# Norming the first token tile by itself at the start of a two-layer trunk, with its loads in another order

## The reference

```python
def layer_norm(x, g, b, eps=1e-5):
    mu = mean(x); var = mean((x - mu) ** 2)
    return (x - mu) * rsqrt(var + eps) * g + b

h = layer_norm(x, ln_in_g, ln_in_b)
for l in range(DEPTH):
    proj = h @ w_in[l]          # 1024 x N_IN, then the three mixers
    ...
```

## Time and profile before

| | before |
|---|---|
| median of 3 runs | 1507.97 us (1507.71 to 1509.43) |
| span of the profiled execution, first to last instruction | 1504.3 us |
| PE busy | 1442.3 us, 96% |
| DVE busy | 752.0 us, 50% |
| ACT busy | 584.0 us, 39% |
| read from HBM | 471.53 MB, 314 GB/s over the span |

### The profile page before, as it was taken

One profiled execution on the slowest core, in us unless ns is written; L12 is line 12 of the kernel. 1 busy time (PEld: TensorE's weight loads), 2 busy tenths in 40 slices (PEclk: granted clock), 3 DMA queues, 4 the chain that ended last, 5 costly groups with the idle time before them and its releaser, 6 DMA issues.

```text
span 1504.3 us, 17635 instructions
## 1 busy us (share of the span) xinstructions
PE 1442.3 (96%) x7456; PEld 993.6 (66%) x7456; DVE 752.0 (50%) x791; ACT 584.0 (39%) x621; POOL 13.3 (1%) x18
## 2 busy tenths in 40 slices
PE   8999999999999999999999899999988999999876
PEld 7987888888888988886343478863423688734223
DVE  7449687555557548674112079941110598510103
ACT  4357665344335357751100067730000577400001
POOL 1000010000000000010000000000000000000000
PEclk9999999999999999999999999999999999999999
DMA  9253275555554353289999999999999999999995
GB/s 358 108 224 126 98 252 204 187 193 179 187 196 168 113 224 127 98 333 430 430 430 429 428 431 430 429 406 431 429 431 430 429 431 428 420 430 431 429 430 228
DMA packets 43245, 473.70 MB, mean 315 GB/s; under 512 B 5424, under 2 KB 5552, under 8 KB 7712
## 3 DMA queue, kind: packets, MB, share of 16 engines
q1 hardware_dynamic: 42336, 467.97, 76.6%
q0 software_dynamic: 832, 4.63, 0.8%
HBM read 471.53 MB, written 1.05 MB: 314 GB/s over the span
## 4 chain that ended last, share of the span: by engine, by line
PE 68%; DMA 17%; DVE 9%; ACT 4%; issue 2%; DVEq 0%; SPq 0%; ACTq 0%
PE ps L1939 15%; PE ps L1940 15%; PE ps L1941 15%; PE ps L2366 12%; DMA raw_b<-in_w_item 11%; DMA raw_a<-in_w_item 6%; PE ps L2403 5%; DVE lo_a L1233 2%; PE ps L2323 1%; ACT w_hi L847 1%; PE ps L2373 1%; ACT prob_even L966 1%; PE ps L1969 1%; DVE small_mix L1449 1%; DVE lo_b L1656 1%
## 5 line engine op out<-in xcount | busy, mean ns | idle before, releaser
L1233 DVE TENSOR_TENSOR lo_a<-raw_a,w_hi 128x2048 fp32r<-128x2048 f32 (+1 forms) x109 | 239.9, 2211 | 120.6 <-ACT w_hi L847 120.0
L1939 PE MATMUL ps<-w_hi,act_hi 128*128 128x512 f32 (+1 forms) x640 | 246.1, 385 | 2.7 <-DVE act_lo L1347 1.1
L847 ACT ACTIVATE w_hi<-raw_a 128x2048 fp32r<-128x2048 f32 (+1 forms) x109 | 200.8, 1848 | 114.2 <-PE ps L1941 113.9
L1941 PE MATMUL ps<-w_hi,act_lo 128*128 128x512 f32 (+1 forms) x640 | 242.5, 379 | 0.0
L1940 PE MATMUL ps<-lo_a,act_hi 128*128 128x512 f32 (+1 forms) x640 | 242.5, 379 | 0.0
L2366 PE MATMUL ps<-raw_a,x_small 128*64 128x512 f32 (+1 forms) x784 | 150.7, 534 | 7.3 <-DMA raw_a<-in_w_item 7.3
L2366 PE MATMUL ps<-raw_b,x_small 128*64 128x512 f32 (+1 forms) x704 | 140.2, 546 | 9.5 <-DMA raw_b<-in_w_item 9.5
L1135 ACT ACTIVATE hidT<-ps 128x512 f32<-128x512 f32 (+1 forms) x24 | 13.0, 544 | 324.3 <-PE ps L2373 324.3
L1939 PEld LDWEIGHTS ps<-w_hi,act_hi 128*128 128x128 f32 x640 | 120.4, 188 | 27.7 <-issue 2.1
L1941 PEld LDWEIGHTS ps<-w_hi,act_lo 128*128 128x128 f32 x640 | 120.4, 188 | 23.0
L1940 PEld LDWEIGHTS ps<-lo_a,act_hi 128*128 128x128 f32 x640 | 120.5, 188 | 21.2
(11 more groups left out here) (293 smaller groups left out, 1905.1 us busy)
## 6 DMA issues: line engine op xcount, KB each, us to landing
raw_a<-in_w_item SPq DMA_DIRECT2D x83, 2048.0 KB, 22.0
raw_b<-in_w_item SPq DMA_DIRECT2D x81, 2048.0 KB, 22.6
raw_a<-in_w_mix SPq DMA_DIRECT2D x60, 1024.0 KB, 4.9
raw_a<-in_w_item SPq DMA_DIRECT2D x43, 1024.0 KB, 5.1
raw_a<-in_w_mix SPq DMA_DIRECT2D x8, 512.0 KB, 3.7
ln_gb<-in_ln_mix POOLq DMA_DIRECT2D x2, 1024.0 KB, 5.6
raw_x<-in_w_item SPq DMA_DIRECT2D x1, 2048.0 KB, 17.3
raw_act<-in_w_item SPq DMA_DIRECT2D x1, 2048.0 KB, 19.7
```

What stands on the lines that cost most here:

```text
L847: nc.scalar.activation(w_upper(g)[:, 0:n], raw(slot)[:, 0:n], ACT.Copy).then_inc(s_hi, 1)
L1233: nc.vector.tensor_tensor(w_lo(slot)[:, 0:n], raw(slot)[:, 0:n], w_upper(g)[:, 0:n].bitcast(F32), ALU.subtract).then_inc(s_lo, 1)
L1939: nc.tensor.matmul(dst, xh, wh, start=start, stop=False)
L1941: return nc.tensor.matmul(dst, xl, wh, start=False, stop=stop)
```

## The change

SP issues tile 0 of x, the identity, `ln_gb`, weight unit 0 and then tile 1 of x; units 1 to 3 follow. DVE computes statistics, variance and refinement for tile 0 alone and normalises it, and only then does statistics and variance of tile 1 (`first_statistics(1)`), all of it ahead of the lower part of tile 0. The refinement for tile 1 stands in `first_normalise(1)`, at its old place. ACT takes two roots of one column each; the second stands between the pieces 1 and 2 of unit 0. PE's order is as before.

```diff
             sp.dma_start(ident, consts[:, 0:P]).then_inc(s_id, 16)
+            sp.dma_start(ln_gb[:], ln_in.rearrange("(o m) d -> o m d", o=1).to_broadcast([P, 2, D])).then_inc(s_gbf, 16)
+            first_load(0)
             sp.dma_start(h[:, 1, :], x[0, P:2 * P]).then_inc(s_x[1], 16)
-            sp.dma_start(ln_gb[:], ln_in.rearrange("(o m) d -> o m d", o=1).to_broadcast([P, 2, D])).then_inc(s_gbf, 16)
-            for k in range(4):
+            for k in range(1, 4):
                 first_load(k)
...
             act.wait_ge(s_idle, 1)
             ready_root()
-            root(TILES)
+            root(1)
             transposed_hi(0, act_hi, (0,))
             first_split(0)
             first_split(1)
+            root(1)
             transposed_hi(0, act_hi, (1,))
...
+            def first_statistics(t):
+                dve.wait_ge(s_x[t], 16)
+                for b in range(2):
+                    statistics(h, t, b)
+                link(nc.vector.bn_aggr(mv[:, t, :], bst[:, t].rearrange("p c m -> p (c m)")))
+                nc.vector.tensor_scalar(rv[:, 0:1], mv[:, t, 1:2], 1e-5, 0.25, ALU.add, ALU.mult).then_inc(s_rv, 1)
+
             def first_normalise(t):
                 halves = [slice(0, 512), slice(512, 1024)]
+                refine(1, rn[:, t:t + 1])
+                dve.wait_ge(s_gbf, 16)
                 for cols in halves:
...
-            for t in range(TILES):
-                dve.wait_ge(s_x[t], 16)
-                for b in range(2):
-                    statistics(h, t, b)
-                link(nc.vector.bn_aggr(mv[:, t, :], bst[:, t].rearrange("p c m -> p (c m)")))
-            nc.vector.tensor_scalar(rv[:, 0:TILES], mv[:, :, 1], 1e-5, 0.25, ALU.add, ALU.mult).then_inc(s_rv, 1)
-            refine(TILES, rn[:, 0:TILES])
-            dve.wait_ge(s_gbf, 16)
+            first_statistics(0)
             first_normalise(0)
+            first_statistics(1)
             transposed_lo(0, act_hi, act_lo, (0,))
```

## The result

| | before | changed |
|---|---|---|
| median, first measurement | 1508.07 us (11 runs, 1505.92 to 1509.43) | 1512.14 us (11 runs, 1508.35 to 1514.06) |
| ratio, 95% interval, first measurement | | 1.0020 (1.0011 to 1.0029) |
| second measurement, another chip | 1508.54 us (29 runs) | 1511.18 us (12 runs), 1.0018 (1.0009 to 1.0027) |
| third measurement, a third chip | 1508.10 us (35 runs) | 1510.48 us (12 runs), 1.0016 (1.0005 to 1.0027) |
| span of the first profile | 1504.3 us | 1510.9 us |

The changed kernel is slower, by 2.4 to 3.0 us by the three ratios (0.0016 to 0.0020 of 1508). The forecast was +1.0, 1509.0 with a range up to 1510.5; the first median, 1512.14, lies outside of it.

What follows compares the result with a forecast made beforehand. PE was taken to bound the kernel, so a late start counts in full. Landing of tile 1 of x plus 6.24 put its norm 0.98 us late: span 1504.3 + 1.0 = 1505.3, plus 3.67 gives 1509.0 us, range 1507.7 to 1510.5.

Steps and rivals of the forecast that it cites:

- the gain on tile 0: On DVE, tile 0's normalising begins at 8.25 us instead of 9.96, 1.7 us earlier.
- the block of six: Six DVE instructions from the first `act_lo` to tile 1's second refinement, taken to last 3.61 us.
- the step that carries the delay one to one: No engine has room behind the start, so a late start moves both later stages by the same time.
- it lands at 8.15 to 8.6, I take 8.2: Landing of `ln_gb` in the new load order, in us, with 1.64 MB up to its end.
- I take 11.9, the measured landing of exactly those bytes: Landing of tile 1 of x, in us, closing the same five transfers that weight unit 0 closed before.
- The late bound of 12.35 for the landing: Tile 1 of x landing 1.45 us behind its bytes, at 12.35 us; the sum is then +1.4 us.
- the term "landing": Landing of tile 1 of x, taken as 11.9 us; tile 1's norm on DVE starts 6.24 us after it.
- the lowest run (-0.3): Lower end of the range, from a start level with the kernel before and the lowest run: 1507.7 us.
- The first (an early landing): Tile 1 of x lands by or before the end of tile 0's norm; +0.2, 1508.2 us, chance 0.15.
- the fourth (the earlier tile 0 wins): The stream is set by tile 0's products, not tile 1's norm; 1.4 us gained, 1506.6 us, chance 0.04.
- The second (absorbed later): A fixed resource behind the start ends last and absorbs the delay; 1508.0 us, chance 0.07.
- The third (the clock falls): PE, idle 2.6 us ahead of the first product, drops to its lower clock; +3.7, 1511.7 us, chance 0.04.

Runs made afterwards that it cites:

- late_stats: The changed kernel with tile 1's statistics and variance moved behind the four pieces of unit 0, ACT's second root behind its piece 3; ratio 1.0021 to the kernel before.
- order_only: The changed order on DVE and ACT, with the loads in the order of the kernel before; ratio 1.0007 to the kernel before.
- x_fourth: The changed kernel with tile 1 of x issued ahead of weight unit 0, behind `ln_gb`; ratio 1.0002 to the kernel before.
- after_third: The changed kernel, not edited, measured a third time; ratio 1.0016 to the kernel before.
- loads_only: The loads in the changed order, with the order on DVE and ACT of the kernel before; 1513.8 us, ratio 1.0032 to the kernel before.
- before_again: The kernel before, not edited, measured and profiled again; ratio 1.0006.
- split_refine: Loads as before; each tile refined separately, both refinements and tile 1's statistics placed in DVE's idle times; ratio 1.0005 to the kernel before.

## Why the prediction was wrong

**Right: what decides.** The stream's start is set by tile 1's norm on DVE; the gain on tile 0 is lost; a wait of 0.8 us for tile 1 of x stands ahead of its statistics (0.78 measured); the block of six takes 3.6, the refinement 0.65 (3.60 and 0.64). The sign was right, and so was the step that carries the delay one to one, as far as 523 us. That the wait came out although both landings were missed is no luck: tile 1 of x lands 3.6 to 3.7 us behind `ln_gb` in all seven profiles with the new loads, tile 0's norm takes 2.87 of this, and in the six with the new order on DVE the wait is 0.71 to 0.79.

**Wrong: the landings, of `ln_gb` and with it of tile 1 of x.** The steps "it lands at 8.15 to 8.6, I take 8.2" and "I take 11.9, the measured landing of exactly those bytes" failed. In the seven profiles with the new loads (late_stats apart, where they stand elsewhere) its statistics start between 12.15 and 13.92, 12.97 on average; 11.97 was the estimate. The late bound of 12.35 for the landing was too tight as well. In the four profiles with the first five transfers in the old order and 1 MB of `ln_gb` the fifth lands at 11.9 to 12.7. So the same bytes in another order land later, by some 0.7 us on average, though the two ranges overlap and the profiles are few; the runs do not show the reason. The other 0.35 is that the profile used was the earliest of the four. All of it is there at `ln_gb`, which closes the first 1.64 MB: 8.45 to 10.15 us in the seven profiles, 9.2 on average, where 8.2 was taken.

**Wrong: the sum, in consequence.** Tile 1's norm starts at 18.16 to 19.93 in the profiles with the new loads and the changed order on DVE, 18.90 on average over the six with tile 1's statistics in the changed place: 1.75 us late, not 0.98. At equal clock the changed kernel is 1.7 and 1.8 us slower in its two paired measurements, and about 2.4 in the first by the pooled level of before (1503.9 against 1506.3). The mechanism was right and the term "landing" was mis-sized, by 1.4 us in the first profile and by about 0.9 on average over the six; the terms behind it, 6.24 in the sum, were 0.15 too long, since statistics and variance take 1.77 and not 1.90.

**Wrong: what the loss was put down to.** The prediction spoke of the wait and of what is queued behind it. order_only and x_fourth show that the wait itself is the smaller part, 0.86 us: the statistics, variance and refinement of tile 1 were hidden in the time in which DVE waited for `ln_gb` anyway, and the change put them on the path. From norm to norm it takes 9.66 us instead of 7.19, which is 2.47 more: 1.77 for statistics and variance, 0.64 for the refinement, 0.78 for the wait, less the 0.71 of idle time ahead of the first `act_lo` that they fill. Against that stands the earlier start of tile 0's norm, 0.34 us in the first profile and up to 1.39 in after_third (8.57).

**Wrong: the range.** It took the noise from three runs that were 1.7 us apart and from one profile with a mean clock of 0.998. That step ("the lowest run (-0.3)", "the upper spread of the runs") failed: the kernel's runs spread over 7 us, with the granted clock. Of the 4.1 us between the first two medians, some 2 are the start. By the 0.49 another 0.7 is clock (10.8 us lost in the 11 changed runs, 9.3 on average over the 99 of the kernel before); the granted clock of the runs it was paired with is not known. The rest is chance as far as is known: the means of the same runs are only 3.5 us apart, and later pairs 2.6 and 2.4 at the median. Whether a part of it belongs to the change (the changed kernel lost 10.8, 10.2 and 10.7 us of clock time, the kernel before 9.6, 8.9, 9.5, but 10.8 in before_again) is left open: it would be worth about 0.5 us.

**The rivals.** The first (an early landing) and the fourth (the earlier tile 0 wins) did not come. The second (absorbed later) holds in part: loads_only was 6.9 us late at tile 1's norm and 5.2 at the end on average, and the profiles regain 1.3 to 4.1 us behind 746 us. For the changed kernel itself it did not help: 1.75 us late at the norm, 1.7 and 1.8 slower at equal clock. The third (the clock falls) had 0.04 and came in one profile of three, at a price of 0.5 us at the stream, not 3.7, since the waits for DVE hid most of it. The page on the clock gate ("TensorE: Matmul & The Clock Gate", "Part 1: The HAM clock gate", of the Trainium skill) says that idle time lets the clock fall; the traces agree that it can after 2.38 us (2.48 in late_stats, 7.6 in loads_only), and show that it need not after 2.38 or 3.23.

## What to carry to other kernels

Before you split a joint step so that the first part can start early, look at what the joint step was hidden behind: here one engine computed both tiles' statistics while it waited for a load anyway, and splitting put 2.4 us of its work and a wait onto the path, 2.5 more in all between the two norms, to win at most 1.4. If you split, place each new piece in a named idle time of that engine (split_refine: level, where the change lost 2). And take the noise from many runs with their granted clock; three runs and one profile can all be lucky.

## What the runs showed of the hardware

- The granted clock differs between executions of one kernel, and that is most of its spread: 0.49 us for each microsecond of clock time lost. That a whole microsecond costs only half fits the profiles: before_again loses 7.7 us between 683 and 746 us, at a clock of 0.79 from 680 to 720 us, and is 3.6 late at the end. That it regains the rest because the transfers bound that stage (99% busy) is argued, not shown.
- PE's clock fell after 2.38 us of idle time in one execution, after 2.48 in late_stats and in loads_only's 7.6, and did not after the same 2.38 us in another, nor after 3.23 us.
- In one profile the big loads of the start land one behind another at the pace of the transfers: tile 1 of x 3.6 to 3.7 us behind `ln_gb` with 1.57 MB between them, which is 420 to 430 GB/s, whether `ln_gb` lands at 8.45 or at 10.15 us. What varies is when the first of them land.
- A transfer does not land by its bytes alone. Five transfers of 3.2 MB together were complete at 11.9 to 12.7 us in one order and at 12.1 to 13.9 in another; 512 KB of `ln_gb` at the fourth place landed at 10.2 us, in an execution that was late ahead of it too, while the whole 1 MB at that place had landed at 9.4 to 10.2.
